# Moving the second block's work to other slots of a merged schedule, with a lag of 1 instead of 4

## The chip, the cores and the metric

One core of a Trainium2 chip runs the whole program. The metric is the device time of one execution in microseconds; lower is better.

## What is computed

The reference is a chain of two transformer-like blocks on 256 tokens of width 1024, in float32, each of depth 2. The first block has feed-forward layers, a recurrent mixer and cross attention. The second, where the change lies, has for each of its two layers attention with a rotary embedding, and then a mixture of 16384 tiny experts (PEER): each token picks 8 x 16 = 128 experts, and

```python
def peer_block(hb, w_q, sub_keys, u_tab, v_tab):
    q = (hb @ w_q).reshape(n, PEER_HEADS, PEER_QDIM)
    ...
    v1, i1 = lax.top_k(s1, PEER_TOPK)
    v2, i2 = lax.top_k(s2, PEER_TOPK)
    ...
    u = u_tab[expert]
    act = jax.nn.gelu(jnp.einsum('nhkd,nd->nhk', u, hb).astype(jnp.float32))
    w = (g * act).astype(hb.dtype)
    return jnp.einsum('nhk,nhkd->nd', w, v_tab[expert])
```

Before that each layer does `x = x + g1 * (o @ w_o)` with the attention's output `o`, and a normalisation with modulation gives `hb`.

## The kernel before

The tokens are handled as two blocks of 128 (`FIRST_BLOCK`, `LAST_BLOCK`), one token on each of 128 partitions. In the stage of interest, `weighted_sums(l)`, called once for each layer l, the experts' rows are fetched and summed. Its unit is a slot: slot n of 256 (128 for the first block of tokens, then 128 for the second) handles one expert of each of 128 tokens.

What happens in a slot, on four engines:

- GpSimd issues an indirect gather (L546): for each token the expert's row of u and v together, 2048 floats, 8 KB, into one of `PAIRS` = 7 places of `ring`. From slot 7 on it first waits for `pair_used`, which TensorE raises when it has finished the pair 7 slots earlier. It also waits for the indices (`idx_done`) at the first slot of each part of the search.
- VectorE (`dot`, L1863) multiplies the u half with `h_tm` and sums it: one number for each token.
- ScalarE (`gelus`) applies gelu, multiplies with the gate, and builds a diagonal matrix from it (`diags`, 3 places). Gelu and exponential use different function tables, so a switch between them brings a table load.
- TensorE multiplies that diagonal with the v half and accumulates in `ps_a` (L910 for slots 0 to 127, L914 for the others).

Between the slots of the first block of tokens, the rest of the work of the second block is interleaved by hand. Each engine has a function `second_block(n)`, called after its part of slot n, which looks up in tables of slot numbers what to do. The engines take their instructions strictly in this order:

- attention in four units of two heads: `ATT_SCORES` (TensorE, L819 to L825), `ATT_MAX` (maximum on VectorE, then exponentials on ScalarE), `ATT_OVER` (VectorE's reciprocal; then TensorE's product with the weights, L833), `ATT_PV` (two copies on ScalarE, then the product with the values, L844) and `ATT_OUT` (ScalarE copies the result). `ATT_OUT` waits for `pv_done` of the same unit; `ATT_OVER` waits for the exponentials.
- `WO_SLOTS`: 8 chunks of the output projection (L863), each a 512 KB weight tile. `B1_ADD` adds the result (VectorE, then squares on ScalarE), `B1_MEAN` on TensorE (L597), `B1_STD` on ScalarE, `B1_NORM` on VectorE and ScalarE (eight modulations).
- `PQ_SLOTS`: 16 chunks of the query projection (L759). ScalarE takes each group of four (`query_take`) `LAG` slots after its last chunk. `B1_TM` copies the transposed tokens.
- `B1_SCORES`: two halves of the key scores (L888); the first waits for all groups of queries, ScalarE takes each half `LAG` slots later.

`PEER_PARTS` places the search for the best experts on VectorE in five parts: (block, first head, last head, slots given after each of 15 steps, first slot). Weight tiles are loaded by the sync queue into `wring`, 4 places, as TensorE frees them (`chunk_done`). In the slots 128 to 255 of the first layer, pieces of the next layer are interleaved (`ctx_piece`, unchanged).

Of the kernel before, what the change touches and what calls it, by code (L numbers as in the profile page):

```python
# [52 lines left out]
WR = 4  # L53
MIX_CHUNKS = 64
ADA_CHUNKS, QKV_CHUNKS, WO_CHUNKS, PQ_CHUNKS = 48, 12, 8, 16
# [20 lines left out]
PEER_PARTS = ((0, 0, 2, (0,) * 15, 0),  # L76
              (0, 2, 4, (2, 1, 1, 2, 1) + (1,) * 5 + (1, 2, 2, 2, 1), 0),
              (0, 4, 8, (3, 2, 2, 3, 2) + (3, 2, 2, 3, 2) + (2, 3, 3, 2, 2), 20),
              (1, 0, 4, (2,) * 15, 76),
              (1, 4, 8, (3,) * 15, 106))  # L80
LAG = 4
ATT_SCORES, ATT_MAX, ATT_OVER = (-1, 0, 6, 12), (-1, 5, 11, 17), (0, 7, 13, 19)
ATT_PV, ATT_OUT = (4, 11, 17, 23), (8, 15, 21, 27)
WO_SLOTS = tuple(28 + 4 * i // 3 for i in range(WO_CHUNKS))
B1_ADD, B1_MEAN, B1_STD, B1_NORM = 42, 43, 47, 48
PQ_SLOTS = tuple(49 + 4 * i // 3 for i in range(PQ_CHUNKS))
B1_TM, B1_SCORES = 49 + LAG, (71, 76)
SUMS_OUT, SUMS_BACK = SLOTS + 1, SLOTS + 3
EARLY_PARTS = 1
GATED_AT = {1: 0, 2: 3}  # L90
# [83 lines left out]
def program(nc, a, out):  # L174

    with ExitStack() as ctx:
# [376 lines left out]
        def _(eng):  # L553
# [38 lines left out]
            def mean_of(src, bank, weights, ready, n_ready):  # L592

                for k in range(KT):
                    if k % (KT // n_ready) == 0:
                        eng.wait_ge(ready, pe.next(ready))
                    ins = mm(bank, weights, src[:, k, :], start=k == 0, stop=k == KT - 1)  # L597
                return ins
# [194 lines left out]
            def weighted_sums(l):  # L793
# [18 lines left out]
                def half_scores(h):  # L812
                    g, r0 = h // 2, h % 2 * 2
                    if h:
                        eng.wait_ge(s_exp, pe.next(s_exp))
                    for r in range(2):
                        q, at = qk_n[:, REP * g + r0 + r, LAST_BLOCK], D + 512 * r
                        if l == 1:
                            mm(ps_a[:, at:at + T], q, keys_t[:, g, 0:T], start=True, stop=True)  # L819
                            mm(ps_a[:, at + T:at + 2 * T], q, keys_t[:, g, T:2 * T], start=True, stop=False,  # L820
                               skip_group_check=True)
                            ins = mm(ps_a[:, at + T:at + T + P], ident, window[:, 1, FIRST_BLOCK],
                                     start=False, stop=True, skip_group_check=True)
                        else:
                            ins = mm(ps_a[:, at:at + 2 * T], q, keys_t[:, g, :], start=True, stop=True)  # L825
                    ins.then_inc(s_done, pe.adds(s_done))
# [21 lines left out]
                def second_block(n):  # L848
# [5 lines left out]
                    if n in ATT_SCORES:  # L854
                        half_scores(ATT_SCORES.index(n))
                    if n in WO_SLOTS:
                        j = WO_SLOTS.index(n)
                        if j == 0:
# [7 lines left out]
                    if n == B1_MEAN:  # L866
                        mean_of(sq_b, ps_c[:, LAST_BLOCK], mean_d, sq2_done, 4).then_inc(ms2_done, pe.adds(ms2_done))
                    if n in PQ_SLOTS:
                        i = PQ_SLOTS.index(n)
                        if i == 0:  # L870
# [265 lines left out]
        def _(eng):  # L1136
            ac = Lane(eng)

            def act(out, in_, func, **k):
                return nc.scalar.activation(out, in_, func, **k)  # L1140
# [107 lines left out]
            def query_take(g):  # L1248
                eng.wait_ge(chunk_done, ac.next(chunk_done, WR))
                act(pq_b[:, WR * g:WR * (g + 1), :],  # L1250
                    ps_b[:, (g % 2) * 512:(g % 2 + 1) * 512].rearrange("p (j t) -> p j t", t=P),
                    ACT.Copy).then_inc(pq_taken, ac.adds(pq_taken))
# [24 lines left out]
            def weighted_sums(l):  # L1277

                def second_block(n):
# [33 lines left out]
                            ins = act(h_tm[:, 1, 512 * j:512 * (j + 1)], ps_a[:, D + 512 * j:D + 512 * (j + 1)], ACT.Copy)  # L1313
                        ins.then_inc(tm_taken, ac.adds(tm_taken))
                    for g in range(PQ_CHUNKS // WR):
                        if n == PQ_SLOTS[WR * g + WR - 1] + LAG:
                            query_take(g)
                    if n - LAG in B1_SCORES:
                        half = B1_SCORES.index(n - LAG)
                        eng.wait_ge(sc_done, ac.next(sc_done))  # L1320
                        for j in range(2):
                            ins = act(pscore[1][:, PEER_H * half + 4 * j:PEER_H * half + 4 * j + 4, :],
                                      ps_a[:, D + 512 * j:D + 512 * (j + 1)], ACT.Copy)
                        ins.then_inc(sc_taken, ac.adds(sc_taken))
# [24 lines left out]
                def ctx_piece(n):  # L1349
# [16 lines left out]
                    elif n == CTX_DEV:  # L1366
                        eng.wait_ge(qk_ms_done, ac.next(qk_ms_done))
                        act(view(arena, 9216 + 512 * 4, 512), ps_d[:, :], ACT.Sqrt, scale=D / P,
                            bias=eps[:, 1:2]).then_inc(qk_std_done, ac.adds(qk_std_done))

                second_block(-1)
                at = 0
                for b, h0, h1, after, begin in PEER_PARTS[EARLY_PARTS:]:
# [1072 lines left out]
```

## Time and profile before

| | |
|---|---|
| median of 3 runs | 3585.74 us (3584.17 to 3585.98) |
| the profiled execution | 3585.98 us; its span in the profile 3584.2 us |
| mean granted TensorE clock | 0.977 of full speed |
| busy: TensorE | 3231.6 us, 90% |
| busy: VectorE | 2064.9 us, 58% |
| busy: ScalarE | 913.5 us, 25% |
| busy: GpSimd | 1189.5 us, 33% |
| HBM traffic | 324 GB/s over the span |
| gathers of pairs (L546) | 512, from 2026.1 to 3563.0 us |

The span is what the profiler saw from the first instruction to the last; the execution's time has 1.8 us more around it. Engines overlap, so the busy times do not add up to the span. In rows of a timeline the columns are start in us, duration in us, engine, line, operation, output<-input, shapes, and in brackets the idle time before it with what ended it. PE is TensorE, PEld its weight loads, DVE VectorE, ACT ScalarE, POOL GpSimd. L1140 is the line of a helper through which all of ScalarE's activations go. One matrix product in float32 shows as two entries for each 128 x 512 result: a pair of slots 0 to 127 is x4, and x16 is four pairs.

### The profile page before, as it was taken

What the parts mean: (1) busy time and instruction counts of PE and PEld (TensorE: products, weight loads), DVE (VectorE), ACT (ScalarE), POOL (GpSimd) and SP (SyncE); (2) the same over time, 40 slices, a digit from 0 to 9 for tenths busy, and PEclk for the clock granted to TensorE, in tenths of its full rate; (3) what the DMA queues carried; (4) which work ended last, traced back from release to release, by engine and by line L of the source; (5) the groups of instructions that cost most, each with busy time, mean ns of one, the idle gap of its engine ahead of it and who ended that gap; (6) DMA issues with size and microseconds to landing.
All of it is one profiled execution on the core that took longest, in us unless ns stands there. A gap on an engine that the chain in (4) does not pass through costs nothing.

```text
span 3584.2 us, 46520 instructions
## 1 busy us (share of the span) xinstructions
PE 3231.6 (90%) x16381; PEld 2548.0 (71%) x16389; DVE 2064.9 (58%) x4045; ACT 913.5 (25%) x2369; POOL 1189.5 (33%) x1129
## 2 busy tenths in 40 slices
PE   8899999989999999989998799878889778978887
PEld 5688888868878888868876555348777644625777
DVE  6677778445445558445444475775544267477444
ACT  2310022120010022120022244334433244343333
POOL 1003642424435423425400143443430024344332
PEclk9999999989999999999999899999999889999999
DMA  8578987779979967869943699999994379999998
GB/s 335 198 259 328 394 312 252 288 259 352 355 282 385 353 233 242 300 252 375 351 159 113 245 419 418 408 421 395 416 421 184 107 293 417 412 422 421 421 421 365
DMA packets 246943, 1163.12 MB, mean 325 GB/s; under 512 B 27256, under 2 KB 29656, under 8 KB 180720
## 3 DMA queue, kind: packets, MB, share of 16 engines
q0 software_dynamic: 152784, 825.30, 57.3%
q1 hardware_dynamic: 93936, 335.48, 26.0%
q8 instruction: 105, 1.72, 0.2%
q14 instruction: 70, 0.57, 0.0%
q10 hardware_dynamic: 48, 0.05, 0.0%
HBM read 1159.62 MB, written 1.10 MB: 324 GB/s over the span
## 4 chain that ended last, share of the span: by engine, by line
PE 63%; DMA 20%; DVE 5%; ACT 5%; issue 4%; POOL 0%; SPq 0%; ACTq 0%; DVEq 0%; POOLq 0%
DMA ring<-in_peer_uv,idx 19%; PE ps_b L973 16%; PE ps_b L578 9%; PE ps_a L981 8%; PE ps_a L910 6%; PE ps_a L567 5%; PE ps_b L759 4%; PE ps_a L914 3%; ACT arena L1140 3%; PE ps_b L587 3%; PE ps_b L629 2%; DVE arena L1863 1%; PE ps_c L597 1%; ACT wts L1140 1%; PE ps_a L1039 1%
## 5 line engine op out<-in xcount | busy, mean ns | idle before, releaser
L546 POOL DMA_INDIRECT ring<-in_peer_uv,idx x512 | 551.3, 1077 | 1214.0 <-DVE idx L1753 422.0
L1863 DVE SCALAR_TENSOR_TENSOR arena<-ring,h_tm 128x1024 f32<-128x1024 f32 x512 | 624.9, 1223 | 513.5 <-DMA ring<-in_peer_uv,idx 504.0
L508 POOL DMA_INDIRECT ring<-in_peer_uv,idx_now x512 | 564.8, 1103 | 411.5 <-DVE arena L1781 157.7
L973 PE MATMUL ps_b<-x_t,ring 128*128 128x256 f32 x2816 | 622.3, 379 | 1.8 <-ACT x_t L1140 1.0
L914 PE MATMUL ps_a<-arena,ring 128*128 128x128 f32 x4096 | 520.3, 283 | 112.1 <-ACT arena L1140 110.8
L910 PE MATMUL ps_a<-ring,arena 128*128 128x512 f32 x1024 | 487.9, 614 | 118.8 <-ACT arena L1140 118.3
L973 PEld LDWEIGHTS ps_b<-x_t,ring 128*128 128x128 f32 x2816 | 534.3, 190 | 77.5 <-DMA ring<-in_ffn 3.5
L914 PEld LDWEIGHTS ps_a<-arena,ring 128*128 128x128 f32 x4096 | 480.2, 194 | 153.0 <-ACT arena L1140 150.9
L1140 ACT ACTIVATE arena<-ps_b 128x512 f32<-128x512 f32 (+2 forms) x215 | 106.9, 499 | 1411.4 <-PE ps_b L973 772.2
L910 PEld LDWEIGHTS ps_a<-ring,arena 128*128 128x128 f32 x1024 | 184.3, 193 | 371.3 <-ACT arena L1140 210.2
L981 PE MATMUL ps_a<-arena,ring 128*128 128x256 f32 x1408 | 317.6, 379 | 0.0
L1781 DVE SCALAR_TENSOR_TENSOR arena<-ring,h_tm 128x1024 f32<-128x1024 f32 x256 | 299.3, 1220 | 20.3 <-DMA ring<-in_peer_uv,idx_now 17.9
L981 PEld LDWEIGHTS ps_a<-arena,ring 128*128 128x128 f32 x1408 | 267.5, 190 | 36.4
L1140 ACT ACTIVATE wts<-dots 128x1 f32<-128x1 f32 (+1 forms) x514 | 104.1, 203 | 719.7 <-DVE arena L1863 714.6
L2035 DVE SCALAR_TENSOR_TENSOR arena<-ps_b,arena 128x256 f32<-128x256 f32 x88 | 37.3, 424 | 362.5 <-PE ps_b L973 192.7
L1140 ACT ACTIVATE arena<-consts,wts 128x128 f32<-128x128 f32 x512 | 205.5, 401 | 70.9 <-PE ps_a L914 12.8
L759 PEld LDWEIGHTS ps_b<-arena,wring 128*128 128x128 f32 x1536 | 183.3, 197 | 28.8 <-issue 14.3
L1790 DVE SCALAR_TENSOR_TENSOR arena<-ring,stage,arena 128x1024 f32<-128x1024 f32 x160 | 195.1, 1278 | 3.8 <-DMA ring<-in_peer_uv,idx_now 2.5
L578 PE MATMUL ps_b<-x_t,wring 128*128 128x256 f32 x896 | 196.4, 380 | 0.0
L759 PE MATMUL ps_b<-arena,wring 128*128 128x128 f32 x1536 | 184.9, 281 | 12.6 <-ACT arena L1140 10.5
L567 PE MATMUL ps_a<-arena,wring 128*128 128x256 f32 (+1 forms) x896 | 173.2, 356 | 22.8 <-issue 21.0
L578 PEld LDWEIGHTS ps_b<-x_t,wring 128*128 128x128 f32 x896 | 169.0, 190 | 25.8 <-issue 3.5
(258 smaller groups left out, 3196.6 us busy)
## 6 DMA issues: line engine op xcount, KB each, us to landing
ring<-in_ffn SPq DMA_DIRECT2D x264, 512.0 KB
wring<-in_second_w SPq DMA_DIRECT2D x232, 512.0 KB
wring<-in_mix_w SPq DMA_DIRECT2D x128, 512.0 KB
ring<-in_ada_rows POOLq DMA_DIRECT2D x36, 512.0 KB, 5.7
ring<-in_peer_uv,idx_now POOLq DMA_INDIRECT x512
ring<-in_peer_uv,idx POOLq DMA_INDIRECT x512
ring<-in_second_w SPq DMA_DIRECT2D x4, 512.0 KB, 15.6
ring<-in_c_rows POOLq DMA_DIRECT2D x1, 1024.0 KB, 7.5
```

Source lines behind the costliest of these rows:

```text
L508: G.indirect_dma_start(rows[:, s, :], None, table, bass.IndirectOffsetOnAxis(ap=idx_now[:, half, s:s + 1], axis=0)).then_inc(rows_in[s], p ...
L546: G.indirect_dma_start(pairs[:, slot, :, :].rearrange("p c d -> p (c d)"), None, a["peer_uv"], bass.IndirectOffsetOnAxis(ap=idx[:, b, s:s ...
L567: ins = mm(acc_t[:, j, cols], w[:, k * P:(k + 1) * P], src[:, k, cols], start=k == 0, stop=k == KT - 1)
L578: ins = mm(bank[:, t * T:(t + 1) * T], w[:, k * P:(k + 1) * P], src[:, k, :], start=k == 0, stop=k == KT - 1)
L759: ins = mm(ps_b[:, (g % 2) * 512 + t * P:(g % 2) * 512 + (t + 1) * P], w[:, k * P:(k + 1) * P], h2[:, k, cols], start=k == 0, stop=k == KT ...
L910: ins = mm(ps_a[:, j * 512:(j + 1) * 512], diags[:, at % DIAGS, :], pairs[:, at % PAIRS, 1, j * 512:(j + 1) * 512], start=False, stop=n == ...
L914: ins = mm(ps_a[:, b * D + k * P:b * D + (k + 1) * P], pairs[:, at % PAIRS, 1, k * P:(k + 1) * P], diags[:, at % DIAGS, :], start=False, s ...
L973: ins = mm(bank[:, part * T:(part + 1) * T], fw[:, ft % 2, part, k * P:(k + 1) * P], x_t[:, k, :], start=k == 0, stop=k == KT - 1)
L981: ins = mm(acc_t[:, j, :], fw[:, ft % 2, 2, j * P:(j + 1) * P], hidden[:, ft % 2, :], start=False, stop=last, skip_group_check=True)
L1140: return nc.scalar.activation(out, in_, func, **k)
L1781: V.scalar_tensor_tensor(acc[s % 2], rows[:, s, :], 1.0, h, ALU.mult, ALU.mult, accum_out=out).then_inc(row_used, ve.adds(row_used))
L1863: V.scalar_tensor_tensor(products[n % 2], pairs[:, at % PAIRS, 0, :], 1.0, h_tm[:, n // SLOTS, :], ALU.mult, ALU.mult, accum_out=dots[:, n ...
```

## The change

Only slot numbers change. The attention's four units are packed into slots -1 to 14 instead of -1 to 27, the output projection takes every second slot from 15 to 29 (before three chunks in four slots, 28 to 37), the addition and normalisation take slots 31 to 34 (42 to 48), the query projection every second slot from 36 to 66 (49 to 69), the scores slots 69 and 71 (71 and 76). The lag with which ScalarE takes TensorE's results is 1 slot instead of 4. The last two parts of the search start 3 slots earlier.

```diff
--- before.py
+++ after.py
@@ -76,15 +76,14 @@
 PEER_PARTS = ((0, 0, 2, (0,) * 15, 0),
               (0, 2, 4, (2, 1, 1, 2, 1) + (1,) * 5 + (1, 2, 2, 2, 1), 0),
               (0, 4, 8, (3, 2, 2, 3, 2) + (3, 2, 2, 3, 2) + (2, 3, 3, 2, 2), 20),
-              (1, 0, 4, (2,) * 15, 76),
-              (1, 4, 8, (3,) * 15, 106))
-LAG = 4
-ATT_SCORES, ATT_MAX, ATT_OVER = (-1, 0, 6, 12), (-1, 5, 11, 17), (0, 7, 13, 19)
-ATT_PV, ATT_OUT = (4, 11, 17, 23), (8, 15, 21, 27)
-WO_SLOTS = tuple(28 + 4 * i // 3 for i in range(WO_CHUNKS))
-B1_ADD, B1_MEAN, B1_STD, B1_NORM = 42, 43, 47, 48
-PQ_SLOTS = tuple(49 + 4 * i // 3 for i in range(PQ_CHUNKS))
-B1_TM, B1_SCORES = 49 + LAG, (71, 76)
+              (1, 0, 4, (2,) * 15, 73),
+              (1, 4, 8, (3,) * 15, 103))
+ATT_SCORES, ATT_MAX, ATT_OVER = (-1, 0, 4, 8), (-1, 2, 6, 10), (0, 4, 8, 12)
+ATT_PV, ATT_OUT = (1, 5, 9, 13), (2, 6, 10, 14)
+WO_SLOTS = tuple(range(15, 31, 2))
+B1_ADD, B1_MEAN, B1_STD, B1_NORM = 31, 32, 33, 34
+PQ_SLOTS = tuple(range(36, 68, 2))
+B1_TM, B1_SCORES = 38, (69, 71)
 SUMS_OUT, SUMS_BACK = SLOTS + 1, SLOTS + 3
 EARLY_PARTS = 1
 GATED_AT = {1: 0, 2: 3}
@@ -1313,10 +1312,10 @@
                             ins = act(h_tm[:, 1, 512 * j:512 * (j + 1)], ps_a[:, D + 512 * j:D + 512 * (j + 1)], ACT.Copy)
                         ins.then_inc(tm_taken, ac.adds(tm_taken))
                     for g in range(PQ_CHUNKS // WR):
-                        if n == PQ_SLOTS[WR * g + WR - 1] + LAG:
+                        if n == PQ_SLOTS[WR * g + WR - 1] + 1:
                             query_take(g)
-                    if n - LAG in B1_SCORES:
-                        half = B1_SCORES.index(n - LAG)
+                    if n - 1 in B1_SCORES:
+                        half = B1_SCORES.index(n - 1)
                         eng.wait_ge(sc_done, ac.next(sc_done))
                         for j in range(2):
                             ins = act(pscore[1][:, PEER_H * half + 4 * j:PEER_H * half + 4 * j + 4, :],
```

## Rows read from the trace of the kernel before

**Rows 1.** Windows: stretch, length; PE, PEld, DVE, ACT, POOL busy; clock, DMA share, GB/s.
```profile
2050.00:2075.00 25.00, 23.72 (x78) 12.41 (x77) 22.38 (x56) 16.84 (x47) 10.22 (x9) 1.00 1.01 421
2250.00:2275.00 25.00, 24.45 (x73) 13.12 (x74) 18.97 (x67) 10.13 (x32) 10.06 (x9) 0.88 0.94 373
2475.00:2525.00 50.00, 45.89 (x338) 43.10 (x338) 20.86 (x36) 20.50 (x64) 17.57 (x16) 1.00 0.93 367
2950.00:2970.00 20.00, 20.00 (x69) 10.93 (x68) 16.19 (x58) 12.94 (x36) 11.07 (x9) 1.00 0.97 388
3120.00:3145.00 25.00, 24.82 (x75) 12.78 (x75) 20.16 (x85) 10.82 (x34) 11.11 (x11) 0.94 0.98 398
```

**Rows 2.** Timeline, TensorE and GpSimd, first layer, slots 71 and 72.
```profile
2250.37 3.78 PE L888 MATMUL ps_a<-subk,arena 128*128 128x128 f32 x16 [4.61 <-ACT arena L1140]
...
2253.95 8.14 PE L910 MATMUL ps_a<-ring,arena 128*128 128x512 f32 x16
...
2257.21 0.94 POOL L546 DMA_INDIRECT ring<-in_peer_uv,idx  x1 [10.23 <-PE ps_a L910]
```

**Rows 3.** Timeline of TensorE, first layer, attention: start, us, instruction, idle before.
```profile
2041.09 7.03 PE L910 MATMUL ps_a<-ring,arena 128*128 128x512 f32 x16
...
2052.64 1.98 PE L910 MATMUL ps_a<-ring,arena 128*128 128x512 f32 x4 [1.07 <-ACT arena L1140]
...
2054.46 1.88 PE L825 MATMUL ps_a<-keys_t,arena 128*128 128x512 f32 x4
...
2056.18 1.88 PE L910 MATMUL ps_a<-ring,arena 128*128 128x512 f32 x4
...
2057.89 1.05 PE L833 MATMUL ps_c<-mem_t,arena 128*128 128x128 f32 x8
...
2059.68 7.03 PE L910 MATMUL ps_a<-ring,arena 128*128 128x512 f32 x16
...
2082.55 1.89 PE L844 MATMUL ps_b<-arena,vals 128*128 128x256 f32 x8
```

**Rows 4.** Timeline of ScalarE, first layer, slots 5 to 8, and slot 48.
```profile
2047.51 1.28 ACT L1140 ACT_TABLE_LOAD   x1
...
2048.80 0.69 ACT L1140 ACTIVATE arena<-ps_a,stats 128x512 f32<-128x512 f32 x1
...
2052.18 0.40 ACT L1140 ACTIVATE arena<-consts,wts 128x128 f32<-128x128 f32 x1
...
2056.00 0.36 ACT L1140 ACTIVATE arena<-ps_b 128x256 f32<-128x256 f32 x1
...
2167.82 3.17 ACT L1140 ACTIVATE arena<-arena,mods,gains 128x128 f32<-128x128 f32 x8
```

**Rows 5.** Timeline, first layer: gather 21 and the dot of slot 21.
```profile
2077.84 0.94 POOL L546 DMA_INDIRECT ring<-in_peer_uv,idx  x1 [2.57 <-PE ps_a L910]
...
2085.53 1.23 DVE L1863 SCALAR_TENSOR_TENSOR arena<-ring,h_tm 128x1024 f32<-128x1024 f32 x1 [0.45 <-DMA ring<-in_peer_uv,idx]
```

**Rows 6.** Timeline, second layer: scores on TensorE, gathers 19 and 21, their dots.
```profile
2915.20 7.03 PE L910 MATMUL ps_a<-ring,arena 128*128 128x512 f32 x16
...
2928.85 0.59 PE L819 MATMUL ps_a<-keys_t,arena 128*128 128x256 f32 x2
...
2931.02 1.88 PE L910 MATMUL ps_a<-ring,arena 128*128 128x512 f32 x4
...
2949.32 0.94 POOL L546 DMA_INDIRECT ring<-in_peer_uv,idx  x1 [2.92 <-PE ps_a L910]
...
2954.32 1.23 DVE L1863 SCALAR_TENSOR_TENSOR arena<-ring,h_tm 128x1024 f32<-128x1024 f32 x1 [0.32 <-DMA ring<-in_peer_uv,idx]
...
2954.57 1.79 POOL L546 DMA_INDIRECT ring<-in_peer_uv,idx  x1 [0.30 <-PE ps_a L910]
...
2960.35 1.22 DVE L1863 SCALAR_TENSOR_TENSOR arena<-ring,h_tm 128x1024 f32<-128x1024 f32 x1
```

**Rows 7.** Window after the long idle time of TensorE in the first layer.
```profile
2252.60:2256.00 3.40, 3.40 (x11) 2.36 (x10) 1.23 (x2) 0.90 (x3) 0.00 (x0) 0.50 1.01 419
```

## The prediction, made before the changed kernel was run

> **What bounds the kernel now.** I read first the page's slices: the change touches one stage only, the sums over gathered pairs, which runs from 2026 to 2723 us in the first layer and from 2901 to the end in the second. Then I cut those stretches into windows of 25 us. In nearly all of them the transfers move 421 GB/s at a DMA share of 1.01, while TensorE, VectorE and ScalarE each have idle time [rows 1] (its first line is from the attention part). So what sets the end is bytes: a gathered pair is 128 rows of 8 KB, 1.05 MB, 2.49 us at 421 GB/s; a chunk of weights is 0.52 MB, 1.25 us. An edit that only moves compute costs nothing as long as the queue of transfers never runs dry, and idle time of the DMA engines is lost for good, because the bytes stay the same.
>
> It ran dry in four places: (421-373)/421 of 25 us = 2.8 us, 6.4 us around 2500, 1.6 us in the second layer's attention, and 1.4 us at 3120 [rows 1]. The first and last of these are one mechanism, once a layer. At slot 71 TensorE waited 4.61 us for ScalarE [rows 2]: the scores of slot 71 need the last group of queries, and ScalarE takes it only at slot 69 + LAG = 73. The gather behind that stall was issued after 10.23 us of idle GpSimd [rows 2].
>
> Whether the queue runs dry is decided by the ring of 7 pairs. Gather n+7 is issued when TensorE is done with pair n, so TensorE may trail the transfers by a limited time. I read that slack off two timelines. In the first layer gather 21 was issued at 2077.84 and its dot began at 2085.53, having waited for the data: 7.69 us [rows 5]. The shortest such time with a waiting dot is 2954.32 - 2949.32 = 5.00 us, in the place where the transfers dipped [rows 6]. So at slot 14 (which releases gather 21) the slack was 2.7 us in the first layer; in the second it was 5.78 - 5.00 = 0.8 us [rows 6]. The attention part already lives at the edge.
>
> **The change part by part.** No instruction and no transfer is added or removed; pieces move to other slots.
>
> *Attention of the second block of tokens*, from 28 slots to 15. First TensorE's work. By starts of consecutive entries [rows 3]: a pair 1.72 us, scores 1.72, weights 2059.68-2057.89 = 1.79, values 1.73 (their entry is 1.89 long, that of the scores 1.88). One unit of attention is 5.24 us; in the second layer its scores take 2.17 [rows 6], the unit 5.69. Before, a unit was spread over about 6 slots: 6x1.72+5.24 = 15.6 us of TensorE for 14.9 us of transfers, nearly balanced. Now it gets 4 slots: 12.1 us for 10.0 us of transfers.
>
> Second, a wait comes in. At slots 2, 6 and 10 ScalarE now does both ATT_OUT (copy of the values, waiting for TensorE's slot 1, 5 or 9) and then the exponentials, before it can make the diagonal of the next slot. The order on ScalarE behind that wait: copy 0.36 us, then a table load, two exponentials, a table load, the gelu and the diagonal. From the start of the first load to the next pair on TensorE the trace has 2052.64 - 2047.51 = 5.13 us [rows 3, 4]. So from the end of the values 5.49 us pass until pair 3, 7 or 11 starts; TensorE has one pair (slot 2, 6 or 10) to fill 1.72 of it and idles 3.77. Before, these two pieces were 3 to 4 slots apart and the same wait was 1.07 us [rows 3]. VectorE queues behind it too (ATT_OVER at slots 4, 8, 12 waits for those exponentials), but its work in four slots is well under 15.9 us: it is busy 22.38 of 25 us over about ten slots now [rows 1].
>
> Laid end to end, first layer: scores of slot 0 end at 2041.09 (as now; the start is untouched). Pair 1 and values: 2044.54. Plus 5.49: pair 3 at 2050.03, pair 4 at 2051.75. Two periods of 4x1.72+5.24+3.77 = 15.89: pair 12 starts at 2083.53. Pair, weights, pair, values, pair: slot 14 ends at 2092.2, gather 21 follows 0.45 later as it does now, at 2092.65. That is 14.8 us later than now; less the slack of 2.7, the DMA engines idle **12.1 us**. Second layer, from 2915.20 with a period of 16.34: gather 21 at 2967.65 instead of 2954.57, 13.1 later, less 0.8: **12.3 us**.
>
> This isn't won back. From slot 15 on TensorE needs 1.72+1.79/2 = 2.6 us a slot and the transfers 2.49+0.62 = 3.1, so they are the limit again and full.
>
> *TensorE's clock.* After the 4.61 us of idling the matmuls of slot 71 took 2253.95-2250.37 = 3.58 us [rows 2], where as many of the same size (the weights) took 1.79 [rows 3], and the granted clock was still at its lower level, 0.50 or 1.2 GHz, up to 2256 [rows 7]. That is 5.6 us at half rate, 2.8 us lost. The change makes six idle times of 3.77 us, between this one and the 1.07 us that cost nothing [rows 3]. Bounds 0 and 2.8 each; I take the middle, 1.4, since 3.77 lies nearer to 4.61 but part of the slow stretch will fall into the idle time itself: 6x1.4 = **8.4 us**. The Trainium skill (TensorE: Matmul & The Clock Gate, Why this matters for your kernels) says the same against this change: idle gaps between bursts of matmuls put the engine back to its lower clock.
>
> The Trainium skill (ScalarE: Activation LUTs, What ACT_TABLE_LOAD costs) adds a drain of about 1.38 us to every switch of tables; here the exponential starts at 2048.80, at the end of the load [rows 4], so the trace does not agree. With the drain each of the six waits would be 2.8 us longer and the sum about 17 us higher.
>
> *WO, B1_ADD to B1_NORM.* WO chunks at every second slot cost nothing (above). MEAN, STD and NORM are now one slot apart. ScalarE is held for two table loads, and then 3.17 us by the modulation [rows 4], some 7 us in which TensorE has two pairs, 3.4: it idles about 3.6. Cover: over slots 15 to 29 the transfers fall behind TensorE by 15x0.5 = 7.5 us, so the ring is full. Nothing, unless that cover is missing: then 3.6 a layer.
>
> *Queries and scores, LAG 1.* The last group is taken at slot 67, before the scores of 69, so the stall of slot 71 is gone: minus 2.8 and minus 1.4 [rows 1]. Queries every second slot need 5.2 us of TensorE for 6.2 us of transfers; the chunk loads of the sync queue follow the use of the chunks and bring the same bytes. ScalarE's waits one slot later are shorter than the slot.
>
> *Search of the first block's later parts*, 3 slots earlier: still far ahead of their gathers (slots 128 and 192). Nothing.
>
> Sum: 12.1 + 12.3 - 2.8 - 1.4 + 8.4 = +28.6 us. The profiled execution took 3585.98 us (span 3584.2), 0.24 above the median of the runs; against it the changed kernel takes 3614.5.
>
> **The rivals.**
> - *No clock drop.* The idle times are too short or the surrounding work dense enough; 1.07 us cost nothing. 3585.98+20.2 = 3606.
> - *A further stall.* The chain at slots 32 to 35 finds no cover in either layer (+7), and every idle time costs the full 2.8 of the clock (+8.4): up to 3630. With only one of them about 3622.
> - *No new wait (not slower).* The point that decides is whether ScalarE's copy at slots 2, 6, 10 really has to wait for the values just computed. If the exponentials are hidden, TensorE's delay at slot 14 is 14.8-11.3 = 3.5 and 13.1-11.3 = 1.8 us, the ring takes 2.7 and 0.8 of it, 1.8 is lost and 4.2 won at slot 71: 3583.6. For it speaks that the transfers stayed full in the first layer though TensorE was 23.72 of 25 us busy [rows 1]; against it, that the program's order on ScalarE is fixed.
> - *Faster.* As the last, and the search that ends 3 slots earlier also removes the 6.4 us dip at 2500: 3577. Against it: in that dip TensorE is the busy engine, not VectorE [rows 1].
>
> **How the numbers follow.** Forecast 0.60 (its own range 3606 to 3622), no clock drop 0.15, a further stall 0.10, no new wait 0.10, faster 0.05. A difference of 0.2%, 7 us, is about what a measurement of this kernel can tell. Slower 0.85, same 0.10, faster 0.05. The range leaves out the two last cases and the far end of the stall: 3600 to 3629.
>
> **What the profile after would show.** Right: in 2040 to 2095 three waits of TensorE on ScalarE of 3 to 4 us, windows well under 421 GB/s there and again around 2920 to 2970; gather 21 near 2093; a granted clock of 0.50 after some of these waits; no wait of 4.6 us before the scores of slot 69; full transfers from slot 15 to 127. Wrong: windows at 421 GB/s throughout the attention slots (the ring hides it), TensorE waits of 1 us, or new dips at slots 31 to 36.

## The result and the profile after

The changed kernel takes 3627.33 us (median of 4 runs, 3625.99 to 3634.06), the kernel before 3584.95 in the same comparison: ratio 1.0121, 95% interval 1.0105 to 1.0138. It is slower by 43.4 us (0.0121 x 3584.95). The forecast was +28.6, 3614.5, with a range of 3600 to 3629.

The profiled execution took 3609.12 us (span 3607.3), about 18 less than the median of the runs. The difference lies ahead of the changed stage, in code that both kernels share: its gather 0 is at 2003.70, that of before at 2026.08. The stage itself is therefore read relative to its own gather 0, and times are compared only as ratios to the kernel before run beside it. From gather 0 to gather 255 the first layer takes 701.2 us where it took 677.8, the second 686.4 where it took 663.7: +23.4 and +22.7, together 46.1.

Lines of the program stand one lower than before (L909 for the pairs, L843 for the values). The windows of the stage after, with busy time of each engine, granted clock of TensorE, DMA share and GB/s last, to be held against [rows 1]; the last two are parts of stretches above:

```profile
2025.00:2050.00 25.00, 17.29 (x48) 9.08 (x48) 14.66 (x42) 14.18 (x36) 5.17 (x5) 0.83 0.72 276
2050.00:2075.00 25.00, 20.67 (x70) 11.23 (x69) 14.45 (x34) 13.64 (x29) 7.35 (x6) 0.90 0.58 210
2075.00:2100.00 25.00, 25.00 (x111) 15.82 (x110) 14.90 (x58) 8.81 (x32) 10.23 (x10) 1.00 0.96 385
2225.00:2250.00 25.00, 21.06 (x88) 12.01 (x89) 10.96 (x23) 9.27 (x28) 7.72 (x9) 1.00 1.02 417
2475.00:2525.00 50.00, 46.39 (x326) 43.49 (x327) 20.75 (x35) 20.11 (x62) 16.70 (x16) 0.97 0.93 366
2925.00:2950.00 25.00, 21.05 (x61) 11.54 (x62) 12.49 (x36) 10.42 (x27) 5.93 (x5) 0.80 0.60 222
...
2029.00:2032.00 3.00, 3.00 (x4) 1.45 (x5) 1.57 (x5) 1.49 (x6) 0.00 (x0) 0.50 0.79 328
2080.00:2085.00 5.00, 5.00 (x25) 3.15 (x24) 2.45 (x10) 2.12 (x9) 2.16 (x3) 1.00 0.81 288
```

The attention now runs at 210 to 276 GB/s where it ran at 421 (in the second layer at 388 and more). The part (421 - GB/s)/421 of a window is time in which the DMA engines had nothing to move; below it is called idle time of the transfers. TensorE idles too, 7.7 and 4.3 us of the first two windows: neither the bytes nor TensorE's own work set the pace there. The clock is at its lower level right after a wait (0.50). Behind slot 71 the old dip of [rows 1] is gone (417). The dip around 2500 costs 6.5 us of idle transfers from 450 to 550 us after gather 0, where it cost 6.4: the earlier search did not remove it.

TensorE's timeline of the first layer shows the waits (idle before an entry in brackets, then its releaser), against [rows 3]:

```profile
2021.51 1.89 PE L843 MATMUL ps_b<-arena,vals 128*128 128x256 f32 x8
2023.23 1.88 PE L909 MATMUL ps_a<-ring,arena 128*128 128x512 f32 x4
2028.97 6.51 PE L909 MATMUL ps_a<-ring,arena 128*128 128x512 f32 x8 [3.85 <-ACT arena L1139]
...
2047.99 5.40 PE L909 MATMUL ps_a<-ring,arena 128*128 128x512 f32 x8 [3.85 <-ACT arena L1139]
...
2065.91 3.40 PE L909 MATMUL ps_a<-ring,arena 128*128 128x512 f32 x4 [3.85 <-ACT arena L1139]
2069.78 1.98 PE L909 MATMUL ps_a<-ring,arena 128*128 128x512 f32 x4 [0.48 <-ACT arena L1139]
...
2127.85 3.78 PE L909 MATMUL ps_a<-ring,arena 128*128 128x512 f32 x4 [3.92 <-ACT arena L1139]
...
2141.22 3.70 PE L909 MATMUL ps_a<-ring,arena 128*128 128x512 f32 x8 [2.01 <-ACT arena L1139]
```

There are three waits of 3.85 us, as the prediction laid out (3.77); eight matmuls took 6.51 us after the first and 5.40 after the second, and at full clock 3.70. The period from one wait to the next is 19.02 and 17.92 us, against 15.89 foreseen without a loss of clock. A fourth wait, 3.92 us at 2127.85 (slot 32), was not foreseen.

ScalarE's timeline shows why the third period ends with more than its wait:

```profile
2023.43 0.38 ACT L1139 ACTIVATE arena<-ps_b 128x256 f32<-128x256 f32 x1 [3.71 <-PE ps_b L843]
2023.84 1.28 ACT L1139 ACT_TABLE_LOAD   x1
2025.13 0.69 ACT L1139 ACTIVATE arena<-ps_a,stats 128x512 f32<-128x512 f32 x1
...
2063.54 1.28 ACT L1139 ACT_TABLE_LOAD   x1
2064.83 0.20 ACT L1139 ACTIVATE wts<-dots 128x1 f32<-128x1 f32 x1
...
2065.87 1.28 ACT L1139 ACT_TABLE_LOAD   x1
2067.17 0.23 ACT L1139 ACTIVATE arena<-arena 128x32 f32<-128x32 f32 x1
2067.41 1.28 ACT L1139 ACT_TABLE_LOAD   x1
```

The first three lines are the foreseen chain: copy of the values, load, exponential. Near 2065 a second pair of loads follows one gelu later, for the search's exponentials of 0.23 us. Before, attention and search took theirs within one pair of loads; with the maxima at slot 10 they no longer do. The page of the profile counts 2373 ACT instructions, four more than before.

### The profile page after: what moved, and what is told of

It is laid out like the page before. It is cut to its first block, busy times and chain, and to the rows that moved or that the text cites. A ratio compares the mean times of both kernels' runs of the same rounds, so it can differ in the third digit from the quotient of the medians.

```text
span 3607.3 us, 46532 instructions
## 1 busy us (share of the span) xinstructions
PE 3240.7 (90%) x16389; PEld 2544.4 (71%) x16389; DVE 2065.4 (57%) x4045; ACT 919.6 (25%) x2373; POOL 1174.9 (33%) x1129
## 4 chain that ended last, share of the span: by engine, by line
PE 63%; DMA 20%; ACT 6%; DVE 5%; issue 3%; POOL 0%; SPq 0%; ACTq 0%; DVEq 0%; POOLq 0%
DMA ring<-in_peer_uv,idx 18%; PE ps_b L972 16%; PE ps_a L980 8%; PE ps_b L577 8%; PE ps_a L909 6%; PE ps_a L566 5%; PE ps_b L758 4%; ACT arena L1139 3%; PE ps_a L913 3%; PE ps_b L586 2%; PE ps_b L628 2%; PE ps_c L596 1%; DVE arena L1862 1%; ACT L1139 1%; ACT wts L1139 1%
## 5 line engine op out<-in xcount | busy, mean ns | idle before, releaser
L545 POOL DMA_INDIRECT ring<-in_peer_uv,idx x512 | 540.5, 1056 | 1270.2 <-PE ps_a L909 459.1
L909 PE MATMUL ps_a<-ring,arena 128*128 128x512 f32 x1024 | 507.4, 632 | 156.6 <-ACT arena L1139 156.6
L909 PEld LDWEIGHTS ps_a<-ring,arena 128*128 128x128 f32 x1024 | 187.9, 198 | 424.0 <-ACT arena L1139 265.7
L1139 ACT ACTIVATE arena<-consts,wts 128x128 f32<-128x128 f32 x512 | 205.5, 401 | 81.6 <-PE ps_a L909 22.4
L758 PEld LDWEIGHTS ps_b<-arena,wring 128*128 128x128 f32 x1536 | 181.6, 196 | 27.9 <-issue 14.8
L577 PEld LDWEIGHTS ps_b<-x_t,wring 128*128 128x128 f32 x896 | 169.0, 190 | 25.8 <-issue 3.5
```

The source lines that it names most:

```text
L545: G.indirect_dma_start(pairs[:, slot, :, :].rearrange("p c d -> p (c d)"), None, a["peer_uv"], bass.IndirectOffsetOnAxis(ap=idx[:, b, s:s ...
L577: ins = mm(bank[:, t * T:(t + 1) * T], w[:, k * P:(k + 1) * P], src[:, k, :], start=k == 0, stop=k == KT - 1)
L758: ins = mm(ps_b[:, (g % 2) * 512 + t * P:(g % 2) * 512 + (t + 1) * P], w[:, k * P:(k + 1) * P], h2[:, k, cols], start=k == 0, stop=k == KT ...
L909: ins = mm(ps_a[:, j * 512:(j + 1) * 512], diags[:, at % DIAGS, :], pairs[:, at % PAIRS, 1, j * 512:(j + 1) * 512], start=False, stop=n == ...
```

## The experiments

One table holds what the traces give for each. *Idle* is the idle time of the transfers in us, the sum of (421 - GB/s)/421 times the length over windows laid from gather 0 (25 to 112 us: attention; 112 to 200: WO, norm and queries; 200 to 250: scores of the block), first / second layer. *Later* is the change of the distance from gather 0 to gather 255 against that of before. Each is from one profiled execution; three of the same kernel (after, e1, e16) differ by up to 2 us in the attention column and by 4 in the next. The runs e9 to e12 gave no result; e13 to e16 are the same four kernels.

| run | ratio (95%) | idle, attention | idle, WO to queries | idle, scores | later |
|---|---|---|---|---|---|
| before | 1 | 0.3 / 1.8 | 0.4 / 0.5 | 3.1 / 1.4 | |
| after | 1.0121 (1.0105-1.0138) | 23.4 / 23.8 | 3.0 / 1.6 | 0.2 / 0.1 | 23.4 / 22.7 |
| e1 after again | 1.0132 (1.0115-1.0149) | 21.7 / 24.4 | 5.6 / 4.5 | 0.4 / 0.2 | 25.2 / 24.6 |
| e16 after again | 1.0132 (1.0113-1.0151) | 21.3 / 25.0 | 2.0 / 2.8 | 0.3 / 0.2 | 20.5 / 24.5 |
| e2 LAG 1 alone | 1.000 (0.999-1.001) | 0.3 / 1.7 | 1.7 / 2.2 | 0.2 / 0 | 0.3 / -0.1 |
| e3 output a slot later | 1.0053 (1.0037-1.007) | 7.5 / 12.9 | 3.4 / 3.3 | 0.2 / 0 | 8.5 / 12.3 |
| e4 new wait alone | 1.0086 (1.0069-1.0103) | 16.5 / 18.3 | 0.5 / 2.1 | 1.6 / 2.3 | 15.9 / 18.6 |
| e5 idle time filled | 1.0115 (1.0098-1.0131) | 19.0 / 21.3 | 3.5 / 3.3 | 0.2 / 0.1 | 18.6 / 20.9 |
| e6 norm spaced | 1.0111 (1.0094-1.0127) | 23.7 / 25.8 | 1.5 / 2.2 | 0.2 / 0.2 | 22.4 / 24.1 |
| e7 last take early | 0.9997 (0.9988-1.0006) | 2.0 / 1.3 | 0.5 / 0.5 | 0.6 / 0 | -0.2 / -0.9 |
| e8 e3, shared loads | 1.005 (1.0033-1.0066) | 6.9 / 6.8 | 2.1 / 4.9 | 0.2 / 0 | 6.5 / 8.0 |
| e13 attention alone | 1.0129 (1.0108-1.015) | 22.1 / 24.7 | 1.0 / 0.4 | 0.4 / 0.3 | 20.5 / 22.6 |
| e14 e13, output later, shared loads | 1.0025 (1.0012-1.0037) | 6.3 / 7.1 | 1.0 / 0.5 | 2.1 / 1.9 | 6.7 / 6.4 |
| e15 norm close alone | 1.0002 (0.999-1.0014) | 0.4 / 1.4 | 3.7 / 3.8 | 0.4 / 1.6 | 0.7 / 1.9 |

**The changed kernel again (e1, e16).** No edit.

> The changed kernel once more, since its profiled execution (3609.1 us) was some 17 us under its timed ones (3622 to 3634). Theory (the gap arose ahead of the stage, in code that the change does not touch): time 3622 to 3634, and in the trace gather 21 again 75 to 77 us after gather 0 in both layers (51.8 and 53.5 in the kernel before). Rival (the stage itself varies): those distances differ by 5 us or more from 75.3 and 76.4.

> The changed kernel once more, beside the others of this job. Ratio 1.012 to 1.0135, gather 28 at 92.7 and gather 255 at 701 us after gather 0 in the first layer. If the attention alone carries the loss, the run with the attention's slots alone is within 3 us of it.

3609.93 us beside 3562.58, and 3633.53 beside 3585.77. The ratio repeats, and so does the place of the loss.

**The wait: output one slot later (e3).** The changed kernel with

```
-ATT_PV, ATT_OUT = (1, 5, 9, 13), (2, 6, 10, 14)
+ATT_PV, ATT_OUT = (1, 5, 9, 13), (3, 7, 11, 14)
```

> The changed kernel with ATT_OUT at 3, 7, 11, 14 instead of 2, 6, 10, 14: ScalarE does the exponentials before it waits for the values; the packing stays. Theory (the wait in front of the exponentials makes the idle times of 3.85 us): TensorE's waits fall to about 1 us, gather 21 comes 54 to 58 us after gather 0, time 3580 to 3592. Rival (it is the packing into 15 slots): 3610 or more.

3580.90 us. In this version ScalarE does not have to wait for the values before it makes the exponentials and the next diagonal. TensorE's timeline in the first layer:

```profile
2020.86 3.70 PE L909 MATMUL ps_a<-ring,arena 128*128 128x512 f32 x8 [0.18 <-ACT arena L1139]
...
2046.02 1.98 PE L909 MATMUL ps_a<-ring,arena 128*128 128x512 f32 x4 [0.18 <-ACT arena L1139]
2050.16 1.98 PE L909 MATMUL ps_a<-ring,arena 128*128 128x512 f32 x4 [2.16 <-ACT arena L1139]
```

The three waits fall from 3.85 to 0.18 us and the clock stays up (eight matmuls in 3.70); 2.16 us remain from the second pair of loads. One slot of one list takes away more than half of the loss, so the wait, with the clock that falls after it, is shown to be a cause, and not the only one.

**The wait alone (e4).** The kernel before, spread as it was, with

```
-ATT_PV, ATT_OUT = (4, 11, 17, 23), (8, 15, 21, 27)
+ATT_PV, ATT_OUT = (4, 10, 16, 23), (5, 11, 17, 27)
```

> The kernel before, spread over 28 slots as it was, but ATT_PV at 4, 10, 16, 23 and ATT_OUT at 5, 11, 17, 27, so that ScalarE waits for the values right ahead of the exponentials. Theory (that wait costs by itself, as the stretch is balanced already): three idle times of 3.8 us a layer in place of about 1, and clock drops after them, 10 to 13 us a layer, 3605 to 3611. Rival (only the packing costs): 3585 to 3590.

3594.24 us beside 3562.58. TensorE's timeline:

```profile
2034.34 3.30 PE L910 MATMUL ps_a<-ring,arena 128*128 128x512 f32 x4 [3.85 <-ACT arena L1140]
2055.81 3.43 PE L910 MATMUL ps_a<-ring,arena 128*128 128x512 f32 x4 [3.97 <-ACT arena L1140]
2076.91 6.54 PE L910 MATMUL ps_a<-ring,arena 128*128 128x512 f32 x8 [3.85 <-ACT arena L1140]
```

The same three waits appear with 28 slots of attention, with four matmuls in 3.30 us behind them. The attention's idle time rises by 16.2 and 16.5 us (16.5 - 0.3, 18.3 - 1.8). The prediction's price for waits and clock, 11.3 + 4.2 = 15.5 a layer, holds.

**The packing alone (e8, e14).** The changed kernel (e8), and the kernel before (e14), with the packed slots, the output a slot later and the last unit's maxima at slot 11, where the search takes its exponentials too; e14 leaves WO, norm, queries and LAG 4 as before:

```
+ATT_SCORES, ATT_MAX, ATT_OVER = (-1, 0, 4, 8), (-1, 2, 6, 11), (0, 4, 8, 12)
+ATT_PV, ATT_OUT = (1, 5, 9, 13), (3, 7, 12, 14)
```

> ATT_OUT at 3, 7, 12, 14 (as in the run with ATT_OUT later) and also the last unit's exponentials at slot 11 instead of 10, next to the search's exponentials, so that both share a pair of table loads. Theory (a second pair of loads at slot 11 makes TensorE wait 2.16 us before slot 12): that wait is gone, ratio 1.0045 instead of 1.0053. Rival (the unit is now late for slot 12 and TensorE waits for VectorE there instead): 1.0055 or more.

> The kernel before with the attention's slots of the version that shares a pair of table loads and takes the output one slot after the values (maxima at -1, 2, 6, 11, output at 3, 7, 12, 14); all else as before. Theory: TensorE's own work in four slots, 12.5 us against 10.0 of transfers, is all that is left: some 6.8 us of idle transfers in each layer before gather 41 and none at slots 31 to 44, so ratio 1.0038 where the version with the close chain had 1.005. Rival: the close chain costs nothing of its own, and both have the same ratio, 1.005.

3601.02 us beside 3585.56, and 3595.62 beside 3585.77. ScalarE's timeline of e8 at the third unit: the 0.23 us of the search now stand behind the attention's exponentials, ahead of the load that leads back:

```profile
2066.05 1.28 ACT L1139 ACT_TABLE_LOAD   x1
...
2068.69 0.23 ACT L1139 ACTIVATE arena<-arena 128x32 f32<-128x32 f32 x1
2068.93 1.28 ACT L1139 ACT_TABLE_LOAD   x1
```

TensorE in e14, from one unit to the next (12.55 us for four slots, against the 12.1 worked out and 10.0 of transfers):

```profile
2044.25 3.70 PE L910 MATMUL ps_a<-ring,arena 128*128 128x512 f32 x8 [0.18 <-ACT arena L1140]
...
2056.80 3.77 PE L910 MATMUL ps_a<-ring,arena 128*128 128x512 f32 x8 [0.18 <-ACT arena L1140]
```

and the windows of e14 over 25 to 50 and 50 to 75 us after gather 0:

```profile
2048.60:2073.60 25.00, 24.82 (x93) 14.34 (x92) 21.17 (x55) 17.94 (x44) 10.54 (x9) 1.00 0.93 345
2073.60:2098.60 25.00, 22.05 (x60) 10.11 (x58) 16.51 (x51) 10.46 (x35) 13.21 (x11) 1.00 1.00 393
```

TensorE is busy 24.82 of 25 us at full clock and the transfers still fall to 345 GB/s: here TensorE is the limit. With waits of only 0.18 us and no clock drop the packing costs 6.0 and 5.3 us of idle transfers (6.3 - 0.3, 7.1 - 1.8). Gather 21 comes 4.5 and 5.3 us later after gather 0 than before. The prediction had 3.5 and 1.8 for this delay, and took 2.7 and 0.8 off again as the ring's slack. GpSimd's timeline shows how the gathers leave:

```profile
2048.23 0.94 POOL L546 DMA_INDIRECT ring<-in_peer_uv,idx  x1 [0.78 <-PE ps_a L910]
2053.45 0.98 POOL L546 DMA_INDIRECT ring<-in_peer_uv,idx  x1 [4.28 <-PE ps_a L910]
...
2061.05 1.49 POOL L546 DMA_INDIRECT ring<-in_peer_uv,idx  x1 [0.30 <-issue]
2066.06 0.94 POOL L546 DMA_INDIRECT ring<-in_peer_uv,idx  x1 [3.52 <-PE ps_a L910]
```

Gathers leave in bunches, with 5.22 and 5.01 us between two where weights and scores stand between pairs of TensorE. The transfers start to run dry some 33 us after gather 0, behind gather 12 (2053.45), and not only at gather 21 (2079.88), where the slack was read. But spacing alone does not empty the queue: the kernel before has 4.63 us between two gathers (2082.99 and 2087.62) with transfers at 421 GB/s.

How little the slack meant is seen at gather 18 of e14, issued at 2071.69. Its dot waits for the data and starts 8.09 us later, and yet the transfers are down to 151 GB/s around its issue:

```profile
2079.78 1.23 DVE L1863 SCALAR_TENSOR_TENSOR arena<-ring,h_tm 128x1024 f32<-128x1024 f32 x1 [2.57 <-DMA ring<-in_peer_uv,idx]
```

```profile
2071.00:2073.50 2.50, 2.50 (x13) 1.57 (x12) 2.50 (x7) 0.55 (x2) 1.89 (x3) 1.00 0.63 151
```

**The attention alone, waits included (e13).** The kernel before with only the five attention lists of the changed kernel (two lines of the change).

> The kernel before with only the slots of the attention (scores, maxima, values, ATT_OUT) of the changed kernel; WO, the norm, queries, scores of the block and LAG 4 stay as before. Theory: nearly all of the loss is the attention's, so this runs like the changed kernel: 23.5 us of idle transfers in each layer before gather 41, plus the old 2.9 and 1.3 us at slot 71, minus the 2.8 and 1.4 that the close chain at slots 31 to 44 costs: ratio about 1.0125 to 1.014, gather 28 at 92.7 us after gather 0. Rival: the close WO and norm slots feed back into the attention's excess over the prediction's 16.3 us a layer (the ring would have returned its slack): then 1.009, and gather 28 near 85 us.

3632.96 us, beside 3633.53 for e16 in the same job: the attention's slots carry the loss, and all the other edits, closer WO, norm and query slots and LAG 1, come out at about zero together. Gather 28 came 86.2 us after gather 0, near the rival's 85 and not at the theory's 92.7, yet the ratio is the theory's. The position of a gather was a bad measure: where the WO chunks (here from slot 28 on) are not yet moving, the same idle time goes with earlier gathers. Idle time of the transfers is what compares.

e13 also has a say on slot 71, since LAG is 4 in it:

```profile
2279.17 3.78 PE L888 MATMUL ps_a<-subk,arena 128*128 128x128 f32 x16 [5.54 <-ACT arena L1140]
```

The stall is there, longer than before (5.54 us for 4.61), but it costs little: 0.4 us of idle transfers in the table's window and 1.1 from 250 to 450 us, for 3.1 and 0 before; in the second layer 0.3 and 0.4, for 1.4 and 0.

**The clock (e5).** The changed kernel with 14 matmuls of zeros in bf16 added in each of the three new idle times of a layer, into a bank that the next weights overwrite; nothing is left out.

```
+                    if n in ATT_OUT[:3]:
+                        for i in range(14):
+                            mm(ps_c[:, :], zeros[:, 0:P], zeros[:, :], start=True, stop=True)
```

> The changed kernel with 14 extra matrix products of zeros (128 x 512, bfloat16) on TensorE behind the pair of slots 2, 6 and 10, in its idle times; their result is not used. Theory (each idle time brings a stretch at 1.2 GHz that costs 1.8 to 2.9 us more): the granted clock stays up in the attention part, gather 21 comes 67 to 69 us after gather 0 instead of 75 to 76, time 13 to 16 us under the changed kernel, 3612. Rival (the clock costs nothing there, the idle times alone do): 3625 or more.

3603.14 us beside 3562.52. TensorE's timeline and its clock, where the changed kernel had 6.51 and 5.40 us for the same eight matmuls:

```profile
2023.94 3.19 PE L857 MATMUL ps_c<-zeros 128*128 128x512 bf16 x13
2027.96 3.70 PE L912 MATMUL ps_a<-ring,arena 128*128 128x512 f32 x8 [0.83 <-ACT arena L1142]
```

```profile
2028.00:2031.00 3.00, 3.00 (x7) 1.40 (x8) 1.56 (x5) 1.49 (x6) 0.78 (x1) 1.00 0.80 333
```

The granted clock is 1.00 where it was 0.50, and the period falls to 16.22 us (the next unit's pairs start at 2044.18). In the first layer of after, e1 and e16 it is 17.8 to 19.0 us, so that one drop costs TensorE 1.6 to 2.8 us. The attention's idle time is 3.1 us a layer below the mean of after, e1 and e16 (22.1 / 24.4 against 19.0 / 21.3), 6.2 in all; gather 255 comes 4.4 and 3.0 us earlier than their mean, 7.4 in all; by the ratios of e1 and e5 it is 0.0017 x 3562 = 6 us, with intervals that overlap. The prediction had 8.4. The Trainium skill (TensorE: Matmul & The Clock Gate, Why this matters for your kernels) puts a lower clock behind idle gaps between bursts; by the 0.50 after each 3.85 us, and the 1.00 once the gap is filled, the trace agrees.

**LAG (e2), and the last take alone (e7).** The kernel before with

```
-LAG = 4
+LAG = 1
```

and, as e7, with only the last group of queries taken at PQ slot + 1:

```
+                        if n == PQ_SLOTS[WR * g + WR - 1] + (1 if g == PQ_CHUNKS // WR - 1 else LAG):
```

> The kernel before with LAG = 1 and nothing else moved. Theory (attention costs, the lag does not): the stall before the scores of slot 71 goes, the dips at 2255 and 3125 vanish, 3585 - 4 = 3581. Rival (with a lag of 1 ScalarE waits for TensorE in the dense stretch of queries, and holds up the next diagonals): 3590 or more.

> The kernel before with only its last group of queries taken 1 slot after its chunk instead of 4, LAG 4 elsewhere. Theory (the stall ahead of the scores of slot 71 is the wait for that copy, and it costs 2.8 and 1.4 us of idle transfers): no wait of 4.6 us there, 3 to 4 us under the kernel before. Rival (the second scores of slot 76 and VectorE's wait for them take its place, or the same comes back later): within 1 us of the kernel before.

3561.83 us beside 3562.58, and 3583.96 beside 3585.56. Either way the stall at slot 71 is gone: idle 3.1 / 1.4 becomes 0.2 / 0 and 0.6 / 0, and gather 79 comes 8.1 us and 7.1 us earlier after gather 0 in the first layer. But in e2 gather 255 comes when it came before, 0.3 later. In e2 new idle time of 1.3 and 1.7 us lies between WO and queries, and in the first layer 1.4 us more behind 250 us (0.7 up to 450, 0.7 in the dip around 500); in e7 there is none between WO and queries, and its 3.9 us saved, less 1.2 more of idle time in the attention, are within what the timing can tell from nothing. Removing a dip of 3 us need not move the end, and neither version is shown to be faster than the kernel before.

**The close norm (e15, e6).** The kernel before with add, means, deviation and norm slot by slot, where the ring is full; and the changed kernel with the last two a slot later:

```
-B1_ADD, B1_MEAN, B1_STD, B1_NORM = 42, 43, 47, 48     # e15, from before
+B1_ADD, B1_MEAN, B1_STD, B1_NORM = 42, 43, 44, 45
-B1_ADD, B1_MEAN, B1_STD, B1_NORM = 31, 32, 33, 34     # e6, from after
+B1_ADD, B1_MEAN, B1_STD, B1_NORM = 31, 32, 34, 35
```

> The kernel before with B1_STD and B1_NORM at slots 44 and 45 in place of 47 and 48, so that add, means, deviation and norm follow each other slot by slot as in the changed kernel, at a place where the ring is full. Theory: ScalarE and VectorE are held for both at once, and TensorE waits 2 to 4 us; 1 to 3 us of idle transfers in each layer at 100 to 165 us after gather 0, ratio 1.0 to 1.0015. Rival: the wait is that on VectorE's addition alone, which is the same in both kernels; no idle transfers, and the close chain of the changed kernel cost something only because its ring had just been emptied.

> The changed kernel with B1_STD at 34 and B1_NORM at 35 instead of 33 and 34, so that ScalarE and VectorE meet the mean a slot later. Theory (the closely packed normalisation makes the dips 137 to 165 us after gather 0, 2.8 to 5 us a layer, which the prediction had put at nothing): these dips shrink to under 1.5 us, the ratio to the kernel before falls from 1.0132 to 1.011 to 1.012. Rival (the dips come from B1_ADD, or from the query copies): the dips stay at 2.8 us or more, 1.013.

In e15 the clock falls to 0.74 and the transfers to 325 GB/s over 13 us:

```profile
2165.26 3.03 PE L910 MATMUL ps_a<-ring,arena 128*128 128x512 f32 x4 [2.04 <-ACT arena L1140]
2169.85 8.63 PE L910 MATMUL ps_a<-ring,arena 128*128 128x512 f32 x16 [1.56 <-ACT arena L1140]
```

```profile
2165.30:2178.30 13.00, 11.44 (x20) 4.54 (x21) 13.00 (x20) 8.39 (x26) 4.57 (x4) 0.74 0.84 325
```

2.04 + 1.56 = 3.6 us looks like the price that the prediction named for the case without cover. But these are no new waits. The kernel before has two as long at this place, with transfers at 421 GB/s and a clock of 1.00 (2165.13 to 2178.13):

```profile
2158.85 7.24 PE L910 MATMUL ps_a<-ring,arena 128*128 128x512 f32 x16
2167.96 1.98 PE L910 MATMUL ps_a<-ring,arena 128*128 128x512 f32 x4 [1.88 <-ACT arena L1140]
2171.96 1.98 PE L910 MATMUL ps_a<-ring,arena 128*128 128x512 f32 x4 [2.01 <-ACT arena L1140]
```

There they add up to 3.89 us and stand behind a run of four pairs; in e15 they stand ahead of it, and the pairs behind them run slower: 3.03 us for one that took 1.98, 8.63 for four that took 7.24. The idle time of the transfers in that part rises by 3.3 in each layer, though the ring had not just been emptied; the run's time moves by less than it can be measured (1.0002). What of the 3.3 is the order and what the clock, no run separates. In e6 (3624.35 us beside 3585.56) it is 1.5 / 2.2 where after, e1 and e16 have 2.0 to 5.6 / 1.6 to 4.5: too near to call, and its ratio does not differ from theirs. A wait of 3.9 us at slot 32 (2127.85 above) is in e6 too, so it is not the deviation's or the norm's. VectorE's timeline of the changed kernel names its order:

```profile
2120.75 2.15 DVE L1898 SCALAR_TENSOR_TENSOR x_t<-ps_a,mods,x_t 128x128 f32<-128x128 f32 x8
...
2122.95 1.22 DVE L1692 TENSOR_TENSOR arena<-arena 128x1024 f32<-128x1024 f32 x1
2124.20 1.41 DVE L1677 MAX8 arena<-arena 128x8 f32<-128x256 f32 x4
2125.53 1.21 DVE L1862 SCALAR_TENSOR_TENSOR arena<-ring,h_tm 128x1024 f32<-128x1024 f32 x1
```

B1_ADD, now at slot 31, meets a slice of the search, and the next dot starts 4.78 us after the addition; ScalarE's gate and TensorE's pair stand behind it. That this addition makes the wait of 3.9 us is read from the order; no run moved it.

## Why the prediction was right or wrong

The number came out within the range, but near its end: 3627.3 lies above the forecast's own band (3606 to 3622) and 2 us under 3629. Direction, place and mechanism held; of the 43.4 us the sum had 28.6. By its own terms, in us for both layers together, with before's idle time taken off:

| term | predicted | measured in after |
|---|---|---|
| attention, waits and clock | 12.1 + 12.3 + 8.4 = 32.8 | 23.1 + 22.0 = 45.1 |
| WO, B1_ADD to B1_NORM | 0 | 2.6 + 1.1 = 3.7 |
| stall at slot 71 | -4.2 | -2.9 - 1.3 = -4.2 |
| sum | +28.6 | +44.6 (gathers: +46.1, ratio: +43.4) |

In e1 and e16 the attention is 44.0 and 44.2 by the same count, and WO to B1_NORM 9.2 and 3.9.

**What bounds the kernel: right.** Idle time of the transfers, time and the last gather agree here within 3 us, and in the other runs gather 255 of a layer moves with the idle time within 2 us.

**The wait on ScalarE: right in place, count and size.** It is 3.85 us against 3.77, at slots 2, 6 and 10 of both layers (3.94 in the second). e4 shows it alone, e3 without it. The rival without a new wait is out: the trace has it. Even if it had been absent, e8 and e14 show that the kernel would have been slower (1.005 and 1.0025) and not 3583.6. The faster case is out with it: the dip around 2500 stayed.

**The clock: right, and somewhat too dear.** The prediction had 8.4 us; e5 gives 6 to 7.4. The rival of no clock drop falls with the 0.50 of the windows; e5 shows that without it the change is still slow.

**The failed step: the packing and the ring's slack.** The prediction's working put TensorE's excess at gather 21 at 3.5 and 1.8 us and let the ring take 2.7 and 0.8 of it, so that 0.8 and 1.0 a layer were left. e14 measured 6.0 and 5.3. Added to e4's 16.2 and 16.5 this gives 22.2 and 21.8, where the mean of after, e1 and e16 is 21.8 and 22.6 (with before's taken off): the two causes add up. The packing's 11.3 against the 1.8 of the sum is 9.5 of the 12.3 us that the attention term was short.

Two things were wrong. The first is the rows. Counted from gather 0 of the second layer (2899.33), [rows 6] do not show what they are said to show: 2949.32 is gather 20 and 2954.57 gather 22, while the dots at 2954.32 and 2960.35 are those of slots 19 and 21. The gathers that belong to them are these:

```profile
2945.43 0.97 POOL L546 DMA_INDIRECT ring<-in_peer_uv,idx  x1 [2.67 <-PE ps_a L910]
...
2952.83 1.44 POOL L546 DMA_INDIRECT ring<-in_peer_uv,idx  x1 [2.57 <-PE ps_a L910]
```

From issue to dot it is 8.89 us for slot 19 and 7.52 for slot 21, not 5.00 and 5.78. The second layer's gather 21 is thus delayed by 2967.65 - 2952.83 = 14.8 us, as in the first, and TensorE's excess is 3.5 and not 1.8. A gather that found an empty queue, gather 0 of the first layer, took 5.52 us to its dot; against that the slack would be 2.2 and at most 2.0. The two slips nearly cancel: 12.6 + 12.8 us for 12.1 + 12.3. That the sum did not suffer is luck.

The second is the slack itself, and this is what cost. The time from issue to dot at one gather was taken for a reserve. In e14 it is 8.09 us at gather 18, 2.6 over the 5.52 of an empty queue, with transfers down to 151 GB/s. The ring gave nothing back: gather 21 was 4.5 and 5.3 us late, and 6.0 and 5.3 us were idle. The delay itself was larger than 3.5, since four slots took 12.55 us and not 12.1, in which the 0.18 us waits count. Why the reserve fails is not shown; that it is the bunches of gathers, 5 us apart, is an argument that no run tested.

In the changed kernel's own first layer the delay of gather 21 can be followed: 23.5 us, where 14.8 were foreseen for waits and packing and 4.2 a layer for the clock on top. The half-clock weights ahead of pair 1 (1.91 us and 1.44, against 1.18 and 1.06 before) made it start 1.1 later; the three waits with what stands around them added 0.9 (period 16.22 in e5 for 15.89); the clock 4.5 (19.02 + 17.92 - 32.43); the second pair of loads 2.2 (from pair 11 to gather 21 13.08 us for 10.84). Together these are 8.7. In e1 and e16 gather 21 is 21.9 and 22.0 later: they lack the slow weights ahead of pair 1. That second pair of table loads is a step the prediction missed: it counted one pair a unit. In idle transfers it is hard to find, though: the wait for it and the slow clock fall on the same two pairs, and e4 and e14 add up to the changed kernel without it. The loads themselves cost what it took from [rows 4]: the load at 2063.54 ends at 2064.83 with the gelu's start. The drain of 1.38 us that the Trainium skill (ScalarE: Activation LUTs, What ACT_TABLE_LOAD costs) adds to a switch does not show in this trace either: by an estimate from that page's figure the wait would be some 6.5 us, and it is 3.85. Without the second pair of loads (e8 against e3) the attention's idle time is 6.9 / 6.8 for 7.5 / 12.9; the ratios don't differ.

**No dip from slot 15 on: wrong, small.** The transfers did not fill at once: 288 GB/s from 2080 to 2085. Why the ring took ten more microseconds was not tried.

**The chain at slots 31 to 35: wrong.** It was put at nothing, with a full ring as cover. It cost 3.7 us, and 9.2 and 3.9 in e1 and e16. e15 shows that even before's ring does not cover such a chain: 3.3 us of idle transfers a layer. The price named for no cover, 3.6, is near that by luck: it stood for added waits, and the kernel before waits as long there; new are their order and the slower pairs behind them. The wait at B1_ADD was not in the working at all.

**LAG 1: right in place, not in worth.** In the changed kernel the stall is gone and its 4.2 us with it. But in e13, with the attention packed and LAG left at 4, only 1.5 and 0.7 us of idle transfers are left there, so LAG 1 can have won about 2 of the 4.2; the rest went with the attention's slots. In the kernel before, the same edit gave back 3.0 of 4.3 between WO and queries, and its time did not move.

**A further stall.** This rival, up to 3630, is nearest to what happened in size. Its stall behind slot 31 came, but most of the excess came from the packing.

## What to carry to other kernels

When a kernel is bound by bytes through a ring of buffers, work out an edit stage by stage as idle time of the transfers, and do not subtract a slack that was read at one gather: here none of it came back. Where a reading pairs an issue with a use, count both from the same start; one gather too many changed 8.89 us into 5.00. When pieces are moved together on an in-order engine, write out that engine's queue between the two things that TensorE waits for; here one slot between the copy of the values and the exponentials was worth more than half of the loss. A pair of table loads is shared only as long as its users stay neighbours, so after any move count the loads again.

## What the runs showed of the hardware

How long TensorE waited did not alone decide its clock. Behind 2.01 us it did eight matmuls at full clock (3.70 us, at 2141.22 of the changed kernel); behind 2.04 us, with waits of 1.23 and 1.56 us around it, four took 3.03 us (e15). In the kernel before, waits of 1.88 and 2.01 us, one pair of 1.98 us apart, left the clock at 1.00 (2165.13 to 2178.13). Thirteen recorded matmuls of zeros in bf16, 3 us, inside an idle time of 3.85 kept the granted clock at 1.00 and did not hold up the next pair: 0.83 us of idle time were left before it.
